# Where the token mixer's rounds stand in TensorE's program: mLSTM and attention rounds moved from the head to the middle of a quarter of an in-projection chunk

## What is computed

```
h = x * (1 + scale1) + shift1
(aq, ak, av, ao, gates.., bq, bk, bv, cf_f, cf_b, cq, ci, cg, ga, gb, gc) = split(h @ w_in + b_in)
a_out = sigmoid(ao) * bidirectional mLSTM(aq, ak, av, gates)       # 4 heads of 128, rotary on latent q and k
b_out = softmax attention(bq, bk, bv)                              # 8 heads of 64, local window + cache for g = 1
c_out = rms(bidirectional HGRN2(cf, cq, ci)) * silu(cg)            # 4 heads of 128
y = (sigmoid(ga) * a_out @ w_b[0] + sigmoid(gb) * b_out @ w_b[1] + sigmoid(gc) * c_out @ w_b[2]) @ w_out
x = layer_norm(alpha * x + gate1 * y);  x = layer_norm(alpha * x + gate2 * hier_moe(x * (1 + scale2) + shift2))
```

## The kernel before

| quarter | HGRN round | mLSTM or attention round | after the quarter |
|---|---|---|---|
| 6 / 7 | | max / decay of group 0 | |
| 8 | | | start of the lower bounds (VectorE L1379, GpSimd L1679 to L1685, ScalarE) |
| 10 / 13 | prep / silu of group 0 | | `mod_rows` after 11 |
| 26 / 27 / 28 | out of group 0 / prep of group 1 / none | read_f / read_b / state of group 0 | `mod_rows` after 27 |
| 34 / 35 / 36 | turn / level 0 / level 1 of group 1 | max / decay (with the rotary on GpSimd) / turn of group 1 | `mod_rows` after 35 |
| 43 / 44 | out of group 1 / none | na_scores / na_probs, group 0, first half | `mod_rows` after 43 |
| 46 / 47 | gate of group 0 / none | na_scores / na_probs, group 0, second half | |
| 48 / 49 | gate of group 1 / none | na_out, group 0 / na_turn, group 1 | |
| 50 / 51 / 52 / 53 | | na_cache / na_scores / na_probs / na_out of group 1 | `mod_rows` after 51 |
| 54 / 55 | | na_scores / na_probs of group 1, second half | |

## Time and profile before

### The profile page before, as it was taken

One profiled execution on the slowest core, in us unless ns is written; L12 is line 12 of the kernel. 1 busy time (PEld: TensorE's weight loads), 2 busy tenths in 40 slices (PEclk: granted clock), 3 DMA queues, 4 the chain that ended last, 5 costly groups with the idle time before them and its releaser, 6 DMA issues. The chain is left out here.

```text
span 1688.9 us, 20339 instructions
## 1 busy us (share of the span) xinstructions
PE 1482.9 (88%) x7016; PEld 756.4 (45%) x7016; DVE 594.2 (35%) x1130; ACT 263.4 (16%) x462; POOL 215.9 (13%) x166
## 2 busy tenths in 40 slices
PE   3969889989997899999669697998899969999994
PEld 1426546544443444444224364475444434444441
DVE  1213324432134434343342142344311353443434
ACT  0021211122200111111001112211222011111111
POOL 0152323001200000000002424420121000000000
PEclk9889999999998899999879898999999979999997
DMA  9434323444541799999782434323355247999991
GB/s 400 175 156 162 137 106 119 163 162 155 229 151 37 308 386 385 378 391 378 274 337 106 161 129 163 130 96 146 129 218 221 103 174 299 392 380 379 394 376 42
DMA packets 39938, 381.19 MB, mean 226 GB/s; under 512 B 7866, under 2 KB 11962, under 8 KB 17084
## 3 DMA queue, kind: packets, MB, share of 16 engines
q1 hardware_dynamic: 31536, 377.14, 56.3%
q10 hardware_dynamic: 8332, 3.15, 0.7%
HBM read 376.07 MB, written 4.20 MB: 225 GB/s over the span
## 5 line engine op out<-in xcount | busy, mean ns | idle before, releaser
L812 PE MATMUL psum<-ring,hT 128*128 128x512 f32 x1152 | 527.9, 609 | 35.9 <-POOLq L1627 19.4
L812 PEld LDWEIGHTS psum<-ring,hT 128*128 128x128 f32 x1152 | 218.7, 196 | 292.1 <-issue 269.6
L897 PE MATMUL psum<-ring,tbuf 128*64 128x256 f32 x2048 | 236.5, 385 | 3.1 <-DVE tbuf L1529 3.1
L897 PEld LDWEIGHTS psum<-ring,tbuf 128*64 128x64 f32 x2048 | 146.1, 138 | 109.9 <-issue 46.3
L1388 DVE TENSOR_TENSOR ch<-psum,bias_ring 128x512 f32<-128x512 f32 x72 | 49.7, 691 | 306.2 <-PE psum L812 294.3
L924 PE MATMUL psum<-ring,tbuf 128*64 128x512 f32 x512 | 116.9, 598 | 0.9 <-ACT tbuf L1154 0.9
L1632 POOL TENSOR_TENSOR tbuf<-const,sm 128x512 f32<-128x512 f32 x16 | 16.3, 1041 | 547.6 <-DVE sm L1292 502.1
L1556 DVE TENSOR_TENSOR ch<-ch,psum 128x512 f32<-128x512 f32 x128 | 79.3, 681 | 17.2 <-PE psum L935 13.1
L1535 DVE TENSOR_SCALAR tbuf<-tbuf 128x256 f32<-128x256 f32 x32 | 9.4, 294 | 215.1 <-ACT tbuf L1144 215.1
L627 PE MATMUL psum<-ring,scZ 128*32 128x512 f32 x384 | 54.8, 700 | 32.1 <-DMA ring<-in_stream 27.1
L832 PE MATMUL psum<-ring,tbuf 128*128 128x512 f32 x192 | 82.7, 592 | 0.0
(11 more groups left out here) (266 smaller groups left out, 1314.0 us busy)
## 6 DMA issues: line engine op xcount, KB each, us to landing
ring<-in_stream SPq DMA_DIRECT2D x168, 2048.0 KB, 9.2
bias_ring<-in_b_in SPq DMA_DIRECT2D x36, 256.0 KB, 7.9
ldata<-in_ldata SPq DMA_DIRECT2D x2, 2329.0 KB, 12.9
hbuf<-in_ln SPq DMA_DIRECT2D x4, 1024.0 KB, 7.2
ch<-in_lb_logits SPq DMA_DIRECT2D x2, 1024.0 KB, 16.1
const<-in_const SPq DMA_DIRECT2D x1, 1634.5 KB, 7.4
x<-in_x SPq DMA_DIRECT2D x1, 1024.0 KB, 8.2
out_hgrn<-hbuf ACTq DMA_DIRECT2D x2, 512.0 KB, 3.3
```

Of the source, the lines that this page charges most:

```text
L812: mm = pe.matmul(bank(PJ + g), hT[:, k, g * P:(g + 1) * P], w[:, k, :], start=(k == 0), stop=(k == KT - 1))
L897: mm = pe.matmul(psum[halves_of[hf], j, 0:FE // 2], xgT[:, k, :], w_up(j)[:, k, hf * (FE // 2):(hf + 1) * (FE // 2)], start=(k == 0), stop ...
```

## The change

On TensorE the loop over the quarters no longer calls `in_order`. At the head of a quarter it runs only the HGRN round, and the mLSTM or attention round of the quarter is called when two of its four matmuls have been issued. Each group's accumulation over k goes on across it. The tables `H_AT` and `T_AT`, the rounds themselves, the other engines' code and all transfers are the same, and the other engines still take a quarter's rounds in the same order. Below line 797 the line numbers grow by 2, from the matmul line on by 6 (L812 is L818, L810 is L812, L816 is L822).

```diff
                     if q == T_AT[0]:
                         pe.wait_ge(ldata_loaded, l * 32 + 32)
-                    in_order(h_round, t_round, q)
+                    for n in range(NH):
+                        if H_AT[n] == q:
+                            h_round(n)
                     if q == TURN_AT:
...
                     for k in range(4 * part, 4 * part + 4):
+                        if k % 4 == 2:
+                            for n in range(NT):
+                                if T_AT[n] == q:
+                                    t_round(n)
                         mm = pe.matmul(bank(PJ + g), hT[:, k, g * P:(g + 1) * P], w[:, k, :], start=(k == 0), stop=(k == KT - 1))
```

## The result

| | before | changed |
|---|---|---|
| median of 20 runs each (lowest to highest), us | 1689.56 (1685.57 to 1695.26) | 1693.97 (1691.06 to 1695.93) |
| ratio to before, 95% interval | | 1.0023 (1.0015 to 1.0031) |
| span of the profiled execution | 1688.9 | 1693.8 |
| TensorE busy, and the rest of the span | 1482.9, 206.0 | 1497.6, 196.2 |
| mean granted TensorE clock | 0.949 | 0.938 |

The account below looks back on a forecast made before the run. Experts were taken as bound by the weight stream, in-projections by TensorE and its waits. Terms summed to -1.13 us a layer, -2.3 for two, clock nothing: 1691.53 - 2.3 = 1689.2 us, range 1683.5 to 1696.8.

Parts of the forecast that it names:

- Parts 2 to 5: Per-layer terms: State round (2), Rotary (3), quarters 43 to 50 (4, gain 3.25 us), quarters 51 to 53 (5, loss 2.3).
- Lower bounds: Part 1: decay's matmuls in quarter 7 come later, so the chain to silu's wait ends 1.73 us later a layer.
- State round: Part 2, quarter 28: wait ends 1.1 us late but two matmuls (1.73) run in it, -0.63 us a layer.
- Rotary: Part 3: GpSimd's rotary starts 0.45 us late, turn in quarter 36 comes 1.73 later; its wait nearly goes, -1.28 a layer.
- Quarters 44, 47, 49 and 51: Per layer: quarter 44's transposes come on top, +0.45 us; waits in 47, 49 and 51 shrink or go, -1.73, -0.74, -1.23.
- Quarter 52: TensorE idles 4.1 us waiting for `rows`, with transposes and two matmuls coming after: +2.8 us a layer.
- the waits feared ahead of an HGRN round in quarters 35 to 43: A sign that the forecast was wrong; none expected, since the other engines have over 1 us to spare there.
- so the clock comes to nothing: Slow stretches after idle: -1.7 us at quarters 47 and 36 against 1.7 in one layer of two at quarter 52; net nothing.
- The slower rival: GpSimd follows moved rounds fully, both 4.1 us idles end at low clock: +1.6 waits, +3.5 clock, 1696.6 us; chance 0.17.
- parts 2 and 3: The State round and Rotary gains, 0.63 and 1.28 us a layer; below 1.1 together the change was to lose.
- The fast side: Rival: none of the first layer's low-clock stretches returns and the new idle draws none: 1684.4 us, chance 0.13.
- Splitting the batches: Rival: pairs behind moved rounds run at the low level, 35 rounds a layer costing 1.73 us each: 1813 us, chance 0.02.

Follow-up runs that it names:

- the filled pair: Changed kernel and kernel before, each with unread matmuls added in TensorE's idle time before long waits: 1673.71 us and 1677.8 us.
- the six rounds: Against the kernel before, only the rounds of quarters 28, 36, 47, 49, 53 and 55 moved to the middle of their quarter: 1666.81 us, ratio 0.9863.

## Why the prediction was wrong

**What held.** Parts 2 to 5, all but the lower bounds, were to change the waits by -0.63 - 1.28 - 0.95 = -2.86 a layer; idle outside A changed by -2.94 and -2.91. Idle isn't quite time: four records put behind a wait take 1.98 where they would add 1.72 in a row. By part:

- Lower bounds, +1.73: right. A in the filled pair is 1.5 and 1.85 longer. That the 3.04 only trades time with the 9.72 is right as well: 4.40 and 6.85, with 2.87 of slow records between them that this chain covers, make 14.1 against 12.8. The forecast end of silu's wait, 116.3, came out as 115.47, because the first layer's first matmuls were 1.2 faster; in the second layer the wait ended 72.7 us behind the first matmul for 69.3, decay's low stretch on top of the 1.73.
- State round, -0.63: the idle is 0.90 + 9.22 = 10.12, so -1.04. The wait ended 27.31 us behind the start of C for 26.37, late by 0.9 and not by 1.1, so the gain in time is 0.8.
- Rotary, -1.28: -1.11, GpSimd's end being 0.6 late and not 0.45.
- Quarters 44, 47, 49 and 51, +0.45 - 1.73 - 0.74 - 1.23: the waits are 1.25 (from 0.53), 1.22 (from 2.93), none and none.
- Quarter 52, idle of 4.1 forecast, 4.00 measured; quarter 53 not late. For the whole of E, -0.95 forecast, -0.79 and -0.78 measured.
- None of the waits feared ahead of an HGRN round in quarters 35 to 43 came.

**The step that failed** is "so the clock comes to nothing": the term for TensorE's clock, put at 0, measured +9.3 us of busy time in the two profiles, outside silu's wait, and 7.6 by the medians with and without filled idle. I had balanced one low stretch that goes (quarter 47, -1.7 in one layer: that came true, 3.60 now) against one that comes in one layer of two. In TensorE's busy time the change brought 14.9 us over both layers, of which 5.6 in quarter 12 (6.57 and 6.43 for 3.70) lay under silu's wait. What is left is 9.3 against the forecast 0. Four terms make it:

- Quarter 52, taken at 1.7 in one layer of two: 1.80 and 0.85 on the four records, and 0.86 in both layers on the transposes (1.92 against 1.06), 4.4 in all. I read 4.1 as "nearer to 3.04", which had run at full speed; all eight idles of 4.00 at that place, in four kernels, were followed by the low level.
- State round, taken at 0: 3.75 and 8.34 (3.75 and 8.27 in the second layer) for 3.57 and 7.03, 2.9 in all. I had counted the wait's length and never what follows it.
- Quarter 7 and quarter 55 in the second layer, which were at full speed before (1.95 and 1.06): 3.45 and 1.94 now, and slower records behind them. That is 1.8 and 1.6. Their idle has not changed, 2.31 and 2.98; by the first layer of before such a stretch can be there or not.
- D's one in the second layer, 1.7, behind no idle at all (last section).

They sum to 12.4. Against them stand the 1.7 of quarter 47, 1.2 by which the first matmuls of the first layer happened to be faster (before had them at clock 0.79 behind the start), and 1.3 that E's matmuls take less at full speed (82.25 against 82.89 a layer), which I hadn't counted; silu's records and the first layer's decay add 0.8. That makes 9.0.

The first two are caused by the change: both layers show them, and putting those places back takes them away, but for one layer of ten behind the state round. The last two can differ from one execution to the next, and one profile of each kernel can't tell how much of them belongs to the change. That the medians differ by 4.4, near the 4.9 of the two profiles, speaks for these profiles being typical.

The slower rival came nearest by its difference to before, and by luck. It gave +1.6 for waits (they were a gain of about 4) and 3.5 for the clock (it was 7.6 by the filled pair). Its +5.1 in sum is close to the +4.4 measured, by two errors that cancel. Its threshold was wrong too: without the gains of parts 2 and 3 the terms of a layer sum to +0.78, so the change loses by waits once those two gains fall below 0.78, not 1.1. The fast side asked that no low stretch come back; those behind 2.31 and 2.98 came back, in both layers, and only quarter 47's stayed away. Splitting the batches cost nothing that shows: with rounds between pairs, four records take 1.88 and E at clock 1.00 is shorter with them mixed (91.45) than without (93.15). The Trainium skill (Perfetto Trace Analysis, Matmul Optimizations) wants matmuls back to back in batches, since the engine's power scales with its use. In this case a round within a batch did no such harm (1.88 for four records). Idle did: with it filled, the changed kernel gained 20.3 us.

**And what I did not ask.** I priced a uniform shift and found that a wait between two moved rounds "stays as it is". True, but that is where the gain was given away. With only the waiting ones moved, the time falls by 22.4 us, 19.3 of 23.0 in the in-projections, where the uniform shift lost 4.4.

## What to carry to other kernels

In an in-order stream move the step that waits, not the step it waits for; a shift of both changes nothing between them and makes everything behind the producer late. Price an idle stretch on the busiest engine as its length **plus** the slow work behind it: in these rows 4 us of idle ahead of TensorE cost another 1.7 to 3.1. Where idle can't be removed, unread matmuls in it took 13 us off this kernel as it was before.

## What the hardware showed that I had not expected

- **Length of idle and the low level.** Over the kernels above that were not filled: idle of 2.31 to 2.32 ahead of decay, 7 of 16 cases low (3.3 to 3.6 for four records) and one in between (2.38); 3.03 to 3.06 ahead of quarter 12, 1 of 8; 3.49 there, once, low (5.40 for 3.70); 2.98 ahead of quarter 55, 11 of 14; 4.00 to 4.76 at quarters 12 and 52, 17 of 17. So the same idle is followed by one level here and by the other there, even at one place: length alone doesn't decide between 2.3 and 3.1 us.
- **Low without idle.** Read_f of group 1 has 32 one-column matmul records between others, with no gap. Behind it, in the second layer of before, the eight records took 4.95:

```profile
1112.17 0.36 PE L732 MATMUL psum<-ldata,tbuf 128*128 128x1 f32 x2
1112.39 1.51 PE L734 MATMUL psum<-ch,tbuf 128*128 128x128 f32 x8
1113.70 4.95 PE L812 MATMUL psum<-ring,hT 128*128 128x512 f32 x8
```

  By this alone D lasted 70.8 us in one layer and 74.1 in the other of the kernel before with filled idle. TensorE counts as busy there.
- **Low behind 1.23 us of idle.** With the six rounds moved, the scores of quarter 51 ran at full speed behind their wait and the eight records after them took 5.40, in both layers:

```profile
352.93 1.16 PE L760 MATMUL psum<-tbuf 64*128 64x128 f32 x8 [1.23 <-ACTq L1079]
353.93 1.05 PE L763 MATMUL psum<-tbuf 64*128 64x128 f32 x8
354.91 5.40 PE L822 MATMUL psum<-ring,hT 128*128 128x512 f32 x8
```

  It cost little, since quarter 52's wait of 1.13 was gone in exchange. The kernel with decay moved too shows the same in both layers, and the kernel before with filled idle in one; before, and with quarters 51 and 52 at the head, the eight records took 3.70 behind the same wait. What in the work before draws it is open.
